# A mixture-of-experts block: the second-layer weight chunks go from SyncE's transfer queue to ScalarE's

## The chip, the cores and the metric

One core of one Trainium2 chip runs the whole program. The metric is the device time of one execution in microseconds (us); lower is better. The time before is the median of three runs.

## The reference

The block takes 512 tokens of width 1024, puts 16 meta tokens ahead of them, runs a convolution branch and an mLSTM branch over them and merges both (this first part is not touched by the change). Then comes a mixture of 32 experts, of which each token uses four:

```python
logits = xt @ router_w + router_b
top_val, top_idx = lax.top_k(logits, 4)
gates = softmax(top_val)
...
hcat = xb @ w1[e] + b1[e]                      # w1[e]: 1024 x 2048 float32, 8 MB
h_glu, h_lin = jnp.split(hcat, 2, axis=-1)     # clamped at 7, and at -7 and 7
act = h_glu * jax.nn.sigmoid(1.702 * h_glu) * (h_lin + 1.0)
return act @ w2[e] + b2[e]                     # w2[e]: 1024 x 1024 float32, 4 MB
```

The four results of a token are summed with their gates and added to the residual stream; a last RMS norm gives the output. All 32 experts' weights are read, 12 MB for each, 384 MB in all.

## The kernel before, in words

**The experts' loop.** The experts are worked off in order, one round of a loop for each, with up to 96 token slots for an expert in a pass. The number of passes comes from the data (`n_passes`); in the profiled execution there is one pass, with 32 rounds. The last round stands outside the loops of TensorE, VectorE and GpSimd, because it also starts the final sums.

**The weight ring.** An expert's weights are 12 chunks of 1 MB in 12 fixed buffers (`RING` = 12, L82). Chunks 0 to 7 are first-layer weights (`w1_ring`, `W1C` = 8, 128 rows of w1 each), chunks 8 to 11 second-layer weights (`w2_ring`, 256 rows of w2 each). The trace calls both `w_ring`. In every chunk each of the 128 partitions holds 8 KB that are contiguous in the chip's memory. There is one buffer for each chunk of an expert, so chunk c of the next expert can be asked for once TensorE has used chunk c of this one.

**TensorE's round** (`expert`, L1526 to 1593). It multiplies chunks 0 to 4 one after the other, each for three groups of 32 slots (L1539 to 1548), then two small bias products (L1552, L1558). Then it waits for chunks 5, 6 and 7 together (L1563, L1564) and works them off group by group (L1565 to 1570); this is called the late block below (`LATE` = 3). After that `second(t)` (L1572 to 1586) multiplies by the four w2 chunks, for slot groups 0, 1 and 2. It waits for the four chunks one by one within `second(0)` (L1579), and between `second(0)` and `second(1)` it transposes the next expert's tokens (L1591). A chunk is given free by `ring_used[c]` when its last product is done; for chunk 7 that is `hid_mm`, for chunk 11 `y_mm`. Chunks 8 to 11 are thus given free during `second(2)`, at the end of the round.

**SyncE's queue** (`load_block`, L528 to 536). It asks for the 12 chunks of the next expert in the order 0 to 11, and waits ahead of each for the buffer to be free; the routine that issues is `load_chunk` (L474 to 482, w1 at L478, w2 at L482). All 384 chunks go through SyncE's one hardware queue (q1 in the profile), in the order of the ring. Ahead of the loop the 12 chunks of expert 0 are loaded between other transfers (L488 to 500). SyncE then waits for the slot table (L519), reads it (L521, L524) and loads `last_g` (L526) before the first chunk of expert 1. After the loop it loads the experts' results (`load_results`, L540 to 548), and it has a branch for further passes (L556 to 561).

**ScalarE's round** (L1061 to 1081). It copies two biases out of the banks (L1065, L1067), picks a row (L1068), makes three sigmoids (L1073), waits for the transposes of the next tokens and copies them in two parts (L1080). It issues no transfer in this loop. Its own hardware queue (q10) was used earlier in the program, among others for eight 1 MB stores of zeros into `y_rows` (L884).

**GpSimd** sends each group's results to `y_rows` with an indirect transfer (L740) and gathers the tokens of the expert after next (L706), both through its software queue (q0).

Of the kernel before, what the change touches and what calls it, by code (L numbers as in the profile page):

```python
# [23 lines left out]
P = 128  # L24
# [6 lines left out]
TT = SEQ // P  # L31
# [13 lines left out]
NE = 32  # L45
# [31 lines left out]
TG = SLOTS // 32  # L77
# [4 lines left out]
RING = 12  # L82
W1C = KT
# [25 lines left out]
def hybrid_block(nc, x, meta_tokens, norm_mix_g, w_in, b_in, conv_dw_w, conv_dw_b, conv_ln_g, conv_ln_b,  # L109
# [3 lines left out]
    with ctx:  # L113
# [90 lines left out]
        w1_ring = [at(f"w1_ring{c}", [P, 2, DFF], F32, ring_end - chunk * (c + 1)) for c in range(W1C)]  # L204
        w2_ring = [at(f"w2_ring{c}", [P, 2, D], F32, ring_end - chunk * (W1C + c + 1)) for c in range(RING - W1C)]
# [159 lines left out]
        ring_in = [sem(f"ring_in{c}") for c in range(RING)]  # L365
        ring_used = [sem(f"ring_used{c}") if c not in (W1C - 1, RING - 1) else None for c in range(RING)]
# [3 lines left out]
        y_mm, y_made, y_stored, ffn_step = sem("y_mm"), sem("y_made"), sem("y_stored"), sem("ffn_step")  # L370
# [5 lines left out]
        summed, out_made, out_made_pool = sem("summed"), sem("out_made"), sem("out_made_pool")  # L376
# [41 lines left out]
        def out_parts(i):  # L418

            return [slice(0, D // 2), slice(D // 2, D)] if i == TILE_ORDER[-1] else [slice(0, D)]  # L420

        block = ctx.enter_context(nc.Block())

        @block.sync
        def _(sp):
# [47 lines left out]

            def load_chunk(e, c):  # L474

                if c < W1C:
                    src = expert_w1[0, bass.ds(e, 1), P * c:P * (c + 1), :].rearrange("e p (g n) -> p (e g) n", g=2)
                    sp.dma_start(w1_ring[c], src).then_inc(ring_in[c], 16)  # L478
                else:
                    m = c - W1C  # L480
                    src = expert_w2[0, bass.ds(e, 1), 2 * P * m:2 * P * (m + 1), :].rearrange("e (p k) n -> p (e k) n", p=P)
                    sp.dma_start(w2_ring[m], src).then_inc(ring_in[c], 16)  # L482

            sp.wait_ge(h_lo_made, 2 * TT)
            sp.dma_start(h_res, x[0].rearrange("(i p) d -> p i d", p=P)).then_inc(row_bc_in, 16)
            for c in range(4):  # L488
                load_chunk(0, c)
            load_pair(WO_PAIR, lambda s: w_source(WO_PAIR, s, 0))  # L490

            sp.wait_ge(mm_done, pair_tick(PW_PAIR + 1, 8))
            for c in range(4, 6):
                load_chunk(0, c)
            load_pair(WO_PAIR + 1, lambda s: w_source(WO_PAIR, s, 1))
# [3 lines left out]
            for c in range(6, RING):  # L499
                load_chunk(0, c)  # L500
            sp.dma_start(w_router, router_w[0].rearrange("(k p) e -> p k e", p=P)).then_inc(router_in, 16)
# [25 lines left out]

            def load_block(n, e):  # L528
                for c in range(RING):


                    if c in (W1C - 1, RING - 1):
                        sp.wait_ge(hid_mm if c < W1C else y_mm, n * TG)
                    else:
                        sp.wait_ge(ring_used[c], n)
                    load_chunk(e, c)

# [18 lines left out]
            with sp.If(passes > 1):  # L556
                with sp.Fori(1, passes) as q:
                    with sp.Fori(0, NE) as e:
                        sp.wait_ge(summed, q * TT + TT)
                        load_block(q * NE + e, e)  # L560
                    load_results(q)
# [223 lines left out]
        def _(act):  # L785
# [274 lines left out]
            with act.Fori(0, passes) as q:  # L1060
                with act.Fori(0, NE) as e:  # L1061
                    n = q * NE + e

# [15 lines left out]
                    for m in range(2):  # L1079
                        nc.scalar.activation(xT[:, 4 * m:4 * m + 4], banks[:, m, 0:4 * SLOTS].rearrange("p (k s) -> p k s", s=SLOTS),  # L1080
                                             ACT.Copy).then_inc(xT_made, 1)

            def last_square(m):
# [1047 lines left out]
```

## Time and profile before

| what | value |
|---|---|
| median of 3 runs | 1623.09 us |
| lowest and highest run | 1620.73 and 1624.62 us |
| the profiled execution's own time | 1621.82 us |
| span of its trace | 1620.0 us |
| mean granted clock of TensorE | 0.993 |
| TensorE busy with matmuls | 1580.6 us, 98% of the span |
| SyncE's queue q1 | 464.98 MB, 73.2% of the 16 DMA engines' span |
| chain that ended last | PE 82%, DMA 8%, each other engine 2% or less |

The span runs from the first instruction to the last one; 1.8 us of the execution's own time lie around it. PE is TensorE, DVE VectorE, ACT ScalarE, POOL GpSimd and SP SyncE; a q behind a name is that engine's sequencer, which issues transfers. L1532 is line 1532 of the kernel. "To landing" is the time from the issue of a transfer to the arrival of its last part. A row of a stretch gives its bounds, its length, the busy time of PE, weight loads, DVE, ACT and POOL with the number of instructions, and then TensorE's granted clock, the busy share of the 16 DMA engines (overlapping packets can bring it above 1) and GB/s. A row of a queue gives its packets, MB and the time of its packets as a share of 16 engines.

### The profile page before, as it was taken

The page shows a single profiled execution, that of the slowest core. Times are in us where ns is not written, and L with a number is a line of the kernel's source. Part 1 is how long each engine was busy: PE and PEld are TensorE (multiplying, and loading weights), DVE is VectorE, ACT ScalarE, POOL GpSimd, SP SyncE. Part 2 cuts the span into 40 slices and gives each one's busy share as a digit, 9 for nine tenths or more (in the row PEclk, how much of TensorE's full clock was granted, in tenths as well). Part 3 has the DMA queues.
Part 4 walks back from the last instruction along what each step waited for, and adds up shares of the span by engine and source line. Part 5 has one row for each costly group of instructions (what it writes and reads, how often), then busy time and mean ns, then how long its engine had stood idle before and what let it go on. Part 6 is the DMA issues. An engine that isn't in the chain of part 4 may idle for free.

```text
span 1620.0 us, 38897 instructions
## 1 busy us (share of the span) xinstructions
PE 1580.6 (98%) x16450; PEld 925.2 (57%) x16450; DVE 651.3 (40%) x1245; ACT 395.8 (24%) x605; POOL 427.9 (26%) x465
## 2 busy tenths in 40 slices
PE   6999999998999899999999999999999999999997
PEld 6998988876889634444444444334433444444444
DVE  4799898026241624222422242224222422242247
ACT  5333134255221511111111111111111111111112
POOL 7334334371433621211121112111211121112114
PEclk9999999999999899999999999999999999999999
DMA  7553243320275289999999999999999999999995
GB/s 215 157 182 105 79 144 90 105 78 27 78 298 212 84 300 411 408 409 414 413 408 403 410 411 406 406 409 410 399 409 406 411 395 402 407 411 400 400 416 243
DMA packets 132436, 492.91 MB, mean 304 GB/s; under 512 B 17305, under 2 KB 74817, under 8 KB 82628
## 3 DMA queue, kind: packets, MB, share of 16 engines
q1 hardware_dynamic: 114020, 464.98, 73.2%
q0 software_dynamic: 8736, 16.22, 3.1%
q10 hardware_dynamic: 9632, 11.03, 2.2%
q8 instruction: 35, 0.57, 0.2%
q14 instruction: 13, 0.11, 0.0%
HBM read 476.32 MB, written 24.87 MB: 309 GB/s over the span
## 4 chain that ended last, share of the span: by engine, by line
PE 82%; DMA 8%; POOL 2%; ACT 2%; DVE 2%; SPq 2%; issue 1%; POOLq 0%; DVEq 0%; ACTq 0%
PE banks L1532 36%; PE banks L1104 25%; PE banks L1581 17%; DMA w_ring<-in_expert_w_dram 7%; PE banks L1519 1%; POOL slot_table L693 1%; DVE mix_lo L1898 1%; SPq L442 1%; DMA small<-in_b_in_dram 0%; POOL h_res L759 0%; ACT banks L991 0%; ACT w_hi L800 0%; PE banks L1552 0%; ACT conv L954 0%; SPq L524 0%
## 5 line engine op out<-in xcount | busy, mean ns | idle before, releaser
L1532 PE MATMUL banks<-w_ring,xT 128*32 128x512 f32 x6144 | 671.5, 592 | 4.9 <-DMA w_ring<-in_expert_w_dram 4.0
L1532 PEld LDWEIGHTS banks<-w_ring,xT 128*32 128x32 f32 x6144 | 206.9, 110 | 429.9 <-issue 423.6
L1581 PE MATMUL banks<-w_ring,actT 128*32 128x256 f32 x6144 | 344.6, 380 | 0.0
L1581 PEld LDWEIGHTS banks<-w_ring,actT 128*32 128x32 f32 x6144 | 205.7, 110 | 134.3 <-issue 18.0
L2011 DVE TENSOR_TENSOR hid<-banks,bias 128x512 f32<-128x512 f32 x96 | 63.9, 665 | 477.4 <-PE banks L1532 477.4
L633 POOL TENSOR_TENSOR w_lo<-stage,w_hi 128x2048 fp32r<-128x2048 f32 x38 | 175.2, 4611 | 264.1 <-ACT w_hi L800 264.1
L1104 PE MATMUL banks<-u_hi,w_hi 128*128 128x264 f32 (+1 forms) x528 | 175.6, 333 | 0.3 <-ACT gates L914 0.3
L1104 PE MATMUL banks<-u_hi,w_lo 128*128 128x264 f32 (+1 forms) x528 | 174.6, 331 | 0.0
L1104 PE MATMUL banks<-u_lo,w_hi 128*128 128x264 f32 (+1 forms) x528 | 174.2, 330 | 0.0
L703 POOL COPY token_now<-token_of 96x1 int32 (+1 forms) x33 | 6.1, 183 | 568.7 <-PE banks L1519 564.9
L1065 ACT ACTIVATE bias<-banks 128x512 f32<-128x512 f32 x32 | 19.1, 597 | 560.5 <-PE banks L1552 560.5
L1722 DVE SCALAR_TENSOR_TENSOR banks<-conv_in,taps,banks 128x512 f32<-128x512 f32 x224 | 151.1, 749 | 0.1
L2037 DVE TENSOR_TENSOR y_out<-banks,bias 128x256 f32<-128x256 f32 x96 | 40.7, 424 | 228.5 <-PE banks L1581 228.4
L1104 PEld LDWEIGHTS banks<-u_hi,w_hi 128*128 128x128 f32 x528 | 99.2, 188 | 10.7 <-issue 0.9
L1104 PEld LDWEIGHTS banks<-u_lo,w_hi 128*128 128x128 f32 x528 | 99.2, 188 | 10.0
L1104 PEld LDWEIGHTS banks<-u_hi,w_lo 128*128 128x128 f32 x528 | 99.2, 188 | 9.5 <-issue 0.2
L800 ACT ACTIVATE w_hi<-stage 128x2048 fp32r<-128x2048 f32 x40 | 76.4, 1911 | 101.2 <-PE banks L1104 101.1
L740 POOL DMA_INDIRECT y_rows<-y_out,row_now x93 | 93.7, 1007 | 19.1 <-issue 19.1
L1073 ACT ACTIVATE sig<-hid 128x256 f32<-128x256 f32 x96 | 40.0, 416 | 202.2 <-DVE hid L2012 202.2
L2021 DVE TENSOR_TENSOR act_v<-hid,sig 128x256 f32<-128x256 f32 x96 | 60.5, 630 | 3.3
L712 POOL TENSOR_TENSOR carrier<-carrier 1x1 f32<-1x1 f32 x129 | 26.9, 209 | 95.9 <-DVE y_out L2037 92.4
L728 POOL COPY row_now<-row_of 128x3 int32 x32 | 5.8, 182 | 162.7 <-DMA y_rows<-y_out,row_now 161.4
(298 smaller groups left out, 1626.8 us busy)
## 6 DMA issues: line engine op xcount, KB each, us to landing
w_ring<-in_expert_w_dram SPq DMA_DIRECT2D x384, 1024.0 KB, 22.5
stage<-in_w_in_dram SPq DMA_DIRECT2D x20, 1024.0 KB, 5.3
stage<-in_w_in_dram SPq DMA_DIRECT2D x16, 512.0 KB, 5.3
y_rows<-empty_row ACTq DMA_DIRECT2D x8, 1024.0 KB, 4.7
y_in<-y_rows SPq DMA_DIRECT2D x4, 2048.0 KB, 22.4
stage<-in_conv_pw_w_dram SPq DMA_DIRECT2D x4, 1024.0 KB, 5.1
stage<-in_mlstm_out_w_dram SPq DMA_DIRECT2D x4, 1024.0 KB, 5.1
stage<-in_w_out_dram SPq DMA_DIRECT2D x4, 1024.0 KB, 5.5
```

Of the source, the lines that this page charges most:

```text
L633: nc.gpsimd.tensor_tensor(w_lo[:, s], stage[:, s], w_hi[:, s].bitcast(F32), ALU.subtract).then_inc(w_lo_made[s], 1)
L712: nc.gpsimd.tensor_tensor(carrier[:, 1 + i:2 + i], carrier[:, 0:1], carrier[:, 0:1], ALU.add).then_inc(idx_step, 1)
L740: pool.indirect_dma_start(out=y_dram, out_offset=bass.IndirectOffsetOnAxis(ap=row_now[:, t:t + 1], axis=0), in_=y_out[:, t], in_offset=Non ...
L800: nc.scalar.activation(w_hi[:, s], stage[:, s], ACT.Copy).then_inc(w_hi_made[s], 1)
L1073: nc.scalar.activation(sig[:, t], hid[:, t, 0:GRP], ACT.Sigmoid, scale=ALPHA).then_inc(sig_made, 1)
L1104: last = nc.tensor.matmul(dst, l, r, start=(k == 0 and n == 0), stop=(k == KT - 1 and n == 2))
L1532: last = nc.tensor.matmul(banks[32 * g:32 * (g + 1), t].rearrange("p (c j) -> p c j", j=64), xT[:, k, 32 * t:32 * (t + 1)], units, start=k ...
L1581: last = nc.tensor.matmul(banks[32 * g:32 * (g + 1), 3 + t, 0:GRP], actT[:, t, k], w2_ring[k // 2][:, k % 2, GRP * g:GRP * (g + 1)], start ...
L1722: nc.vector.scalar_tensor_tensor(out=to, in0=src, scalar=taps[:, ct, w:w + 1], in1=acc, op0=ALU.mult, op1=ALU.add).then_inc(conv_step, 1)
L2011: own(nc.vector.tensor_tensor(hid[:, t], banks[:, t], bias1.rearrange("p h n -> p (h n)"), ALU.add))
L2021: own(nc.vector.tensor_tensor(act_v[:, t].rearrange("p (c q j) -> p c j q", q=2, j=32), lin.rearrange("p (c j q) -> p c j q", q=2, j=32), ...
L2037: nc.vector.tensor_tensor(y_out[:, t], banks[:, 3 + t, 0:GRP], bias2, ALU.add).then_inc(y_made, 1)
```

## The change

`load_chunk` is moved out of SyncE's block and takes the issuing engine as its first argument. `load_block` on SyncE now issues chunks 0 to 7 only. ScalarE's round becomes a function `expert(n, e)`; the loop runs over the first 31 experts, and after each round ScalarE waits for the buffers 8 to 11 to be free and issues the w2 chunks of the next expert. The last round stands outside the loop. The 12 chunks of expert 0 are still issued by SyncE, and for a further pass SyncE issues the w2 chunks of expert 0 ahead of that pass. In a single pass, each chunk of experts 1 to 31 waits for the same event as before.

```diff
--- before.py
+++ after.py
@@ -419,6 +419,16 @@
 
             return [slice(0, D // 2), slice(D // 2, D)] if i == TILE_ORDER[-1] else [slice(0, D)]
 
+        def load_chunk(engine, e, c):
+
+            if c < W1C:
+                src = expert_w1[0, bass.ds(e, 1), P * c:P * (c + 1), :].rearrange("e p (g n) -> p (e g) n", g=2)
+                engine.dma_start(w1_ring[c], src).then_inc(ring_in[c], 16)
+            else:
+                m = c - W1C
+                src = expert_w2[0, bass.ds(e, 1), 2 * P * m:2 * P * (m + 1), :].rearrange("e (p k) n -> p (e k) n", p=P)
+                engine.dma_start(w2_ring[m], src).then_inc(ring_in[c], 16)
+
         block = ctx.enter_context(nc.Block())
 
         @block.sync
@@ -471,33 +481,21 @@
                 for j in range(2):
                     load_pair(stage_pair + j, lambda s: w_source(stage_pair, s, j))
 
-            def load_chunk(e, c):
-
-                if c < W1C:
-                    src = expert_w1[0, bass.ds(e, 1), P * c:P * (c + 1), :].rearrange("e p (g n) -> p (e g) n", g=2)
-                    sp.dma_start(w1_ring[c], src).then_inc(ring_in[c], 16)
-                else:
-                    m = c - W1C
-                    src = expert_w2[0, bass.ds(e, 1), 2 * P * m:2 * P * (m + 1), :].rearrange("e (p k) n -> p (e k) n", p=P)
-                    sp.dma_start(w2_ring[m], src).then_inc(ring_in[c], 16)
-
-
-
             sp.wait_ge(h_lo_made, 2 * TT)
             sp.dma_start(h_res, x[0].rearrange("(i p) d -> p i d", p=P)).then_inc(row_bc_in, 16)
             for c in range(4):
-                load_chunk(0, c)
+                load_chunk(sp, 0, c)
             load_pair(WO_PAIR, lambda s: w_source(WO_PAIR, s, 0))
 
             sp.wait_ge(mm_done, pair_tick(PW_PAIR + 1, 8))
             for c in range(4, 6):
-                load_chunk(0, c)
+                load_chunk(sp, 0, c)
             load_pair(WO_PAIR + 1, lambda s: w_source(WO_PAIR, s, 1))
 
             sp.wait_ge(mm_done, pair_tick(OW_PAIR + 1, 8))
             sp.wait_ge(mixed, KT)
             for c in range(6, RING):
-                load_chunk(0, c)
+                load_chunk(sp, 0, c)
             sp.dma_start(w_router, router_w[0].rearrange("(k p) e -> p k e", p=P)).then_inc(router_in, 16)
             sp.dma_start(rb_bc, router_b.to_broadcast([P, NE])).then_inc(router_in, 16)
             sp.dma_start(gf_bc, norm_ffn_g.to_broadcast([P, D])).then_inc(g_in, 16)
@@ -525,15 +523,15 @@
                                  by_slot[32 * t:32 * (t + 1)]).then_inc(rows_in, 16)
             sp.dma_start(last_g, final_norm_g.rearrange("(a d) -> a d", a=1).to_broadcast([P, D])).then_inc(row_bc_in, 16)
 
-            def load_block(n, e):
-                for c in range(RING):
+            def load_block(n, e, chunks=range(W1C)):
+                for c in chunks:
 
 
                     if c in (W1C - 1, RING - 1):
                         sp.wait_ge(hid_mm if c < W1C else y_mm, n * TG)
                     else:
                         sp.wait_ge(ring_used[c], n)
-                    load_chunk(e, c)
+                    load_chunk(sp, e, c)
 
             results = y_dram[0:Y_ROWS].rearrange("(i p r) n -> i p (r n)", i=TT, p=P)
 
@@ -555,6 +553,9 @@
             passes = sp.value_load(n_passes[0:1, 0:1], min_val=1, max_val=PASSES)
             with sp.If(passes > 1):
                 with sp.Fori(1, passes) as q:
+                    sp.wait_ge(summed, q * TT + TT)
+                    for c in range(W1C, RING):
+                        load_chunk(sp, 0, c)
                     with sp.Fori(0, NE) as e:
                         sp.wait_ge(summed, q * TT + TT)
                         load_block(q * NE + e, e)
@@ -1058,8 +1059,7 @@
             act.wait_ge(passes_made, 1)
             passes = act.value_load(n_passes[0:1, 0:1], min_val=1, max_val=PASSES)
             with act.Fori(0, passes) as q:
-                with act.Fori(0, NE) as e:
-                    n = q * NE + e
+                def expert(n, e):
 
                     act.wait_ge(bias_mm, n * 2 + 1)
                     nc.scalar.activation(bias1, banks[:, 3].rearrange("p (h n) -> p h n", h=2), ACT.Copy).then_inc(bias_made, 1)
@@ -1079,6 +1079,17 @@
                     for m in range(2):
                         nc.scalar.activation(xT[:, 4 * m:4 * m + 4], banks[:, m, 0:4 * SLOTS].rearrange("p (k s) -> p k s", s=SLOTS),
                                              ACT.Copy).then_inc(xT_made, 1)
+
+                with act.Fori(0, NE - 1) as e:
+                    n = q * NE + e
+                    expert(n, e)
+                    for c in range(W1C, RING):
+                        if c == RING - 1:
+                            act.wait_ge(y_mm, n * TG + TG)
+                        else:
+                            act.wait_ge(ring_used[c], n + 1)
+                        load_chunk(act, e + 1, c)
+                expert(q * NE + (NE - 1), NE - 1)
 
             def last_square(m):
```

## Rows read from the trace of the kernel before

**Rows 1.** The page: transfers over 40 slices, two queues, issues with us to landing.
```profile
DMA  7553243320275289999999999999999999999995
...
q0 software_dynamic: 8736, 16.22, 3.1%
q10 hardware_dynamic: 9632, 11.03, 2.2%
...
stage<-in_w_in_dram SPq DMA_DIRECT2D x20, 1024.0 KB, 5.3
```

**Rows 2.** The chain that ended last: start in us, length in us, work.
```profile
581.86 22.79 DMA w_ring<-in_expert_w_dram
604.79 7.93 PE banks L1532 x72
...
1026.00 7.73 PE banks L1532 x72
...
1058.23 7.73 PE banks L1532 x72
...
1544.56 7.93 PE banks L1532 x72
...
1577.47 7.73 PE banks L1532 x72
...
1606.16 6.42 POOL h_res L759 x2
```

**Rows 3.** The tile w_ring: what its readers waited for, and time to landing.
```profile
  DMA w_ring<-in_expert_w_dram: 4.0, 5
...
DMA to landing us min/median/max: 7.6/22.5/27.3
```

**Rows 4.** Stretches: all experts; one queue alone; beside GpSimd's. Last: clock, DMA share, GB/s.
```profile
604.00:1577.00 973.00, 970.40 (x11998) 415.88 (x12002) 280.32 (x645) 168.38 (x297) 153.68 (x300) 1.00 1.01 407
...
1018.00:1042.00 24.00, 24.00 (x300) 9.93 (x296) 8.65 (x20) 5.67 (x10) 2.76 (x6) 1.00 1.01 421
1010.00:1017.00 7.00, 7.00 (x96) 2.96 (x92) 0.42 (x1) 0.00 (x0) 2.28 (x4) 1.00 0.99 361
```

**Rows 5.** Timeline of TensorE, 1000 to 1036: start, us; one expert and its neighbours.
```profile
1005.68 7.11 PE L1581 MATMUL banks<-w_ring,actT 128*32 128x256 f32 x128
1012.61 13.06 PE L1532 MATMUL banks<-w_ring,xT 128*32 128x512 f32 x120
...
1025.81 7.91 PE L1532 MATMUL banks<-w_ring,xT 128*32 128x512 f32 x72
1033.54 2.77 PE L1581 MATMUL banks<-w_ring,actT 128*32 128x256 f32 x48
```

**Rows 6.** Timeline of SyncE, 1000 to 1070: start and length of each run of issues.
```profile
1010.40 2.92 SPq L482 DMA_DIRECT2D w_ring<-in_expert_w_dram  x4
1015.57 18.69 SPq L478 DMA_DIRECT2D w_ring<-in_expert_w_dram  x8
```

**Rows 7.** The issue of one last w2 chunk, and its time to landing.
```profile
L482 SPq DMA_DIRECT2D w_ring<-in_expert_w_dram x1: 332/332/332, 1013.0 to 1013.0; - x1
...
DMA to landing us min/median/max: 22.5/22.5/22.5
```

**Rows 8.** Timeline of ScalarE, 1000 to 1030: start, us; idle before.
```profile
1005.79 0.87 ACT L1080 ACTIVATE xT<-banks 128x384 f32<-128x384 f32 x2 [2.50 <-PE banks L1519]
...
1025.93 0.60 ACT L1065 ACTIVATE bias<-banks 128x512 f32<-128x512 f32 x1 [17.97 <-PE banks L1552]
```

**Rows 9.** Queues in the stretch 63 to 66, with both hardware queues at work.
```profile
q1 hardware_dynamic: 872, 0.44, 59.0%
q10 hardware_dynamic: 541, 0.55, 54.4%
```

**Rows 10.** Timeline of SyncE, 566 to 612: chunks for the second expert.
```profile
577.06 5.13 SPq L478 DMA_DIRECT2D w_ring<-in_expert_w_dram  x8
586.79 3.76 SPq L482 DMA_DIRECT2D w_ring<-in_expert_w_dram  x4
```

## The prediction

> **What bounds the kernel now.** I read the page first, for where the transfers are heavy: from the slice at about 600 us on, the 16 DMA engines are at 9 tenths in every slice but the last [rows 1]. That is the experts' loop. Then the chain of waits: it goes through TensorE's blocks, and at its beginning through a weight chunk that is 22.79 us under way and ends in the late block at 604.79 [rows 2]. The late block of the second expert (expert 1) starts at 604.79 and that of the last at 1577.47; that is 972.68 us for 30 rounds, 32.42 us each. The shortest rounds, such as that from 1026.00 to 1058.23, take 32.23 us [rows 2]. I take 32.23 us as TensorE's own round. Waiting for chunks thus costs 972.68 - 30 x 32.23 = 5.8 us in 30 rounds, 0.19 us each. The rows by tile count only 4.0 us in 5 waits [rows 3], expert 1's among them; smaller ones lie within the blocks.
>
> So there are two limits side by side. The windows show the second: from 604 to 1577 the DMA engines are busy for a share of 1.01 [rows 4], never free. With SyncE's queue alone they move 421 GB/s, beside GpSimd's transfers 361 GB/s [rows 4]. A chunk is 1.049 MB, 2.49 us at 421 GB/s; 12 of them take 29.9 us. The rest of the 32.42 us, 2.5 us, goes to GpSimd's stores and gathers. An expert's chunks take as long as TensorE's round, within 1%. Hence the median of 22.5 us to landing [rows 3]: some nine chunks stand in the queue, and one that comes late is made up for by nothing. What counts is the **order** in which they land.
>
> One round by the timelines: it starts at 1012.61, its late block at 1025.81, the second layer at 1033.54 [rows 5]. The four w2 chunks for it were asked for from 1010.40 to 1013.3, the w1 chunks of the next expert from 1015.57 on [rows 6]. The last w2 chunk, issued at 1013.0, lands 22.5 us later, at 1035.5 [rows 7]. TensorE comes to it after 3/4 of a group's second layer (7.11 / 2 = 3.6 us for a group [rows 5]), at 1033.54 + 2.7 = 1036.2: 0.7 us to spare. The late block's chunks are as tight.
>
> **The change, part by part.**
>
> *Issue time.* Four issues a round leave SyncE and go to ScalarE: 2.92 us from the first to the last, most of it waiting between them [rows 6]. SyncE is not late with w1: its next issue is at 1015.57, when chunk 0 comes free, and w2's waits end before that. So freeing it gains 0. On ScalarE what is queued behind the added waits is the bias copy of the next round. ScalarE ends its copies at 1006.7 and idles 17.97 us until 1025.93 [rows 8]; the w2 buffers come free by 1013, so the issues lie in that idle time, with 12 us to spare. Cost 0. If that cover were gone, VectorE's bias additions would be late, then the second layer. Around the end, ScalarE's last round issues nothing. Cost 0 too.
>
> *Order of landing.* Before, a w2 chunk stands behind all w1 chunks issued earlier. Afterwards it stands in q10, which has no backlog, and the DMA engines have two hardware queues to serve. No row has two streams of chunks side by side. The nearest is the stretch 63 to 66, with small packets: q1 takes 59.0% of the engines' time and q10 54.4% [rows 9]. I take equal shares. GpSimd's queue, which gets through in spite of q1's backlog (the rate falls to 361 in its stretch [rows 4]), speaks for the same.
>
> *The start.* SyncE comes late to expert 1: it issues all eight w1 chunks within 577.06 to 582.2, and w2's four from 586.79 on [rows 10]. Chunk 7 lands at 581.86 + 22.79 = 604.65, and TensorE starts its late block right then [rows 2]. At 586.79 w1 has 604.65 - 586.79 = 17.9 us to go, less the fixed part of a landing and GpSimd's share, still over five chunks. The four w2 chunks (9.96 us) therefore all get through on their half before chunk 7 does. Chunk 7 lands 10.0 us later, at 614.6. If TensorE then needs 32.23 us for each of 30 rounds, the last late block starts at 614.8 + 966.9 = 1581.7 instead of 1577.47: **+4.3 us**. The other 5.7 us come back since the chunks have a lead and the small waits vanish.
>
> *The steady state.* Total bytes and rate stay, so the DMA engines are as far as before at each time, unless they idle. At the time chunk 7 is needed, w2 chunks of the same expert have got ahead of it that stood behind it before. How many: w2 is issued from 1010.40, the late block starts at 1025.81 [rows 5, 6], 15.4 us, and both move together with TensorE. Of this take about 2.5 us for the fixed part of a landing (a lone 1 MB load takes 5.3 us [rows 1], less its 2.49) and 2.5 us for GpSimd's traffic, which falls in it: 10.4 us, of which q10 gets half, 5.2 us. So once the lead is used up the schedule lies **+5.2 us** behind that of before. The lead of 5.7 us shrinks by 0.19 us a round, so this limit is reached about the end. It is the larger of the two, and they don't add. The last chunk of w2: 4 x 2.49 x 2 = 19.9 us, plus 2.5 and 2.5, is 24.9 us after 1010.40, 1035.3, needed at 1036.2. No wait there, by 0.9 us.
>
> *The tail.* The results' loads follow TensorE and use the queue behind w1. The chain ends in output sums and scaling (the last long row at 1606.16 [rows 2]), all behind TensorE's last products. I carry the 5.2 us through it whole; from 0 (if loads bound it) to 6.
>
> *Rate.* What two streams do to the rate is the unknown. From below: the row nearest to a loss is 361 against 421 GB/s, 14%, but with small packets and stores [rows 4]; 14% over the some 18 us in which both are busy would be 3 us a round, 90 us in all. From above: a gain could at most remove all waits after the start, which the +4.3 us has already done. I take no loss, because packets of both streams are the same size and kind, and the busy share is 1.01 already. A 1% loss costs 0.18 us a round, some 5 us in all once the lead is gone. The Trainium skill (DMA: Bandwidth & Descriptors, Where 436 GB/s comes from) puts the ceiling of the ports at 435 GB/s. If a second queue filled the gap from the 421 measured, a chunk would take 2.41 us, the first wait 9.6 us, and the sum would be +3.9 instead of +5.2; no row shows this with chunks.
>
> **Sum**: the profiled execution's 1621.82 us + 5.2 = 1627.0. It lies 1.3 us under the median of the runs, so I predict 1623.09 + 5.2 = **1628.3 us**. A measurement of this kernel tells some 0.2% (3.2 us) from no change.
>
> **The rivals.**
>
> *A. Sharing costs rate* (1636 to 1650). If both streams together run 1.5 to 4% below 421 GB/s, 18 us of each round lengthen by 0.3 to 0.7 us, 8 to 22 us, beside the 5.2. For it: the fall to 361. Against: equal packets. Chance 0.19.
>
> *B. w2 becomes the late one* (over 1650). w2 has 0.9 us to spare. If q10 gets 40% and not 50%, its four chunks take 24.9 us instead of 19.9, TensorE waits 4 us for them in a round, and w1 gets ahead; with a full ring the DMA engines then run dry. A share of 45% or less of the time decides. 1 us lost a round is 30 us. For it: the small margin. Against: rows 9, where neither queue is starved. Chance 0.06.
>
> *C. The order doesn't change* (1623.1). If the engines serve chunks by time of issue whatever the queue, q10's wait behind q1's backlog, chunk 7 of expert 1 lands at 604.7, and SyncE's freed time is worth 0, as above. The Trainium skill (DMA: Bandwidth & Descriptors, Issuing engines are not separate DMA queues) says that DMAs of all issuers interleave on the same engines and that issuing from several saves the sequencers' time only; by that alone the sum would be 0. Against it: rows 9 show both at once. Chance 0.12.
>
> *D. Faster* (1617.3). C's order at the start, and the rate of both queues over 0.6% higher, so that the chunks take less than TensorE's 32.23 us: all 5.8 us of waits go. It is decided by whether chunk 7 of expert 1 lands by 604.8. For it: 0.6% is little. Against: needs the order and the gain both. Chance 0.07.
>
> The forecast itself (1625 to 1631) has 0.56.
>
> **How the numbers follow.** The likeliest time is 1628.3. The range from 1622.0 to 1642.0 holds the forecast, C, and the lower half of A, and leaves out D, B and the rest of A, 0.2 or less. Slower by over 0.2%: A, B and most of the forecast (0.81 less 0.04 where it ends just under the bound), 0.77. Same: C and that 0.04, 0.16. Faster: 0.07.
>
> **What would show it.** In the profile after: expert 1's late block starts at about 614.6, released by chunk 7, some 33 us after its issue; w2 chunks land about 9 us (the first) to 22 us (the last) after issue, in q10, which carries some 130 MB more than before; the following rounds take 32.2 us with no DMA wait, w1's times to landing start low and grow; the last late block starts near 1582.5. A start at 604.7 would prove C or D; rounds of 32.6 us or more with a DMA share of 1.01 and below 405 GB/s A; waits ahead of the second layer and a DMA share under 1 B. Any w1 issue that SyncE makes earlier relative to TensorE would prove the first part wrong.

## The result: 9.5 us slower

The median after is 1631.91 us (1630.41 to 1633.92, five runs) beside 1622.40 us (1620.73 to 1624.62, five runs) before. The ratio is 1.0058, with a 95% interval of 1.0044 to 1.0073, so the kernel is slower by 0.4 to 0.7%. The forecast was 5.2 us slower.

The page after, where it answers to [rows 1]:

```profile
span 1632.1 us, 38925 instructions
...
DMA  7553242320275299999999999999999999999994
...
q1 hardware_dynamic: 96164, 334.95, 52.6%
q10 hardware_dynamic: 27488, 141.06, 22.2%
...
L1543 PE MATMUL banks<-w_ring,xT 128*32 128x512 f32 x6144 | 672.8, 593 | 15.6 <-DMA w_ring<-in_expert_w_dram 14.6
...
L729 POOL COPY row_now<-row_of 128x3 int32 x32 | 5.8, 181 | 208.2 <-DMA y_rows<-y_out,row_now 206.9
```

130 MB moved from q1 to q10, and the DMA engines are at 9 tenths from the same part of the span on as before. Work on TensorE is as long as before (its first-layer products are line 1543 here, the second layer is line 1592). What grew is its wait for chunks, and GpSimd's wait for its own stores to land: 206.9 us over 31 rounds, where the same group (line 728 there) had 161.4 us before.

The chain, to be laid beside [rows 2] (start, length, work):

```profile
580.69 32.23 DMA w_ring<-in_expert_w_dram
613.05 9.29 PE banks L1543 x72
...
646.85 7.73 PE banks L1543 x72
...
1324.04 7.97 PE banks L1543 x72
1332.16 24.87 DMA w_ring<-in_expert_w_dram
1357.16 7.97 PE banks L1543 x72
...
1574.03 25.47 DMA w_ring<-in_expert_w_dram
1599.54 1.07 PE banks L1592 x16
```

Chunk 7 of expert 1 is 32.23 us under way instead of 22.79, and the late block waits for it. Then some 22 rounds go through TensorE alone, until chunks come into the chain again from 1332 on. At the very end a w2 chunk is in it, 25.47 us under way. The last late block starts at 1587.33, so the profiled execution can be cut in three:

| part | before | after | difference |
|---|---|---|---|
| to expert 1's late block | 604.79 | 613.05 | +8.26 |
| from it to the last late block, 30 rounds | 972.68 | 974.28 | +1.60 |
| from there to the end of the span | 42.53 | 44.77 | +2.24 |
| span | 1620.0 | 1632.1 | +12.1 |

This execution took 1633.92 us, 2.0 us more than its median, and that of before 0.6 us less than its own; so 12.1 us are seen where the medians differ by 9.5.

TensorE's timeline shows the first and the last part of this (start, length, instructions, idle before):

```profile
613.05 9.29 PE L1543 MATMUL banks<-w_ring,xT 128*32 128x512 f32 x72 [9.85 <-DMA w_ring<-in_expert_w_dram]
...
1599.54 1.07 PE L1592 MATMUL banks<-w_ring,actT 128*32 128x256 f32 x16 [1.71 <-DMA w_ring<-in_expert_w_dram]
```

The late block itself takes 9.29 us instead of 7.93. The stretches tell why (columns as in [rows 4]; last come granted clock, DMA share, GB/s):

```profile
604.00:613.00 9.00, 0.00 (x0) 0.00 (x0) 0.00 (x0) 1.39 (x3) 0.00 (x0) 0.59 1.02 422
613.00:622.00 9.00, 8.95 (x72) 2.81 (x76) 4.50 (x11) 0.83 (x2) 0.00 (x0) 0.84 1.01 422
640.00:1290.00 650.00, 650.00 (x8056) 266.59 (x8052) 182.50 (x420) 113.37 (x200) 102.64 (x201) 1.00 1.01 405
1300.00:1587.00 287.00, 283.55 (x3514) 123.08 (x3510) 83.77 (x192) 46.63 (x83) 46.09 (x90) 1.00 1.00 401
```

While TensorE idles the granted clock falls to 0.59, and it is 0.84 over the late block: part of the block runs at the lower of its two levels, 1.2 GHz. The third line is to be read beside the same 650 us of before, where TensorE was also busy throughout, and the fourth beside the end of the loop before:

```profile
640.00:1290.00 650.00, 649.86 (x8039) 276.40 (x8032) 185.34 (x427) 113.78 (x201) 102.44 (x200) 1.00 1.01 408
1300.00:1577.00 277.00, 275.33 (x3382) 118.72 (x3378) 80.46 (x185) 45.34 (x80) 43.53 (x85) 1.00 1.01 404
```

The DMA engines look full in all four, yet move 405 GB/s instead of 408, and 401 instead of 404 at the end of the loop, where both kernels wait for chunks. By the queues' rows the engines are not quite as busy: the shares of the queues add up to 101.3% before and 100.9% after in the 650 us.

The queues in the 16 us from 590 on, in which both hardware queues have chunks at work:

```profile
DMA packets 1018, 6.73 MB, mean 421 GB/s; under 512 B 166, under 2 KB 166, under 8 KB 226
...
q1 hardware_dynamic: 449, 3.26, 49.0%
q10 hardware_dynamic: 441, 3.23, 48.3%
q0 software_dynamic: 128, 0.25, 4.0%
```

Equal shares, at the 421 GB/s of one queue alone [rows 4].

### The profile page after: what moved, and what is told of

It reads as the page before. It is cut to its first block, busy times and chain, and to the rows that moved or that the text cites. A ratio compares the mean times of both kernels' runs of the same rounds, so it can differ in the third digit from the quotient of the medians.

```text
span 1632.1 us, 38925 instructions
## 1 busy us (share of the span) xinstructions
PE 1579.1 (97%) x16450; PEld 913.0 (56%) x16450; DVE 652.9 (40%) x1245; ACT 392.9 (24%) x603; POOL 428.0 (26%) x465
## 4 chain that ended last, share of the span: by engine, by line
PE 77%; DMA 13%; DVE 2%; ACT 2%; POOL 2%; SPq 2%; issue 1%; POOLq 0%; DVEq 0%; ACTq 0%
PE banks L1543 33%; PE banks L1115 25%; PE banks L1592 16%; DMA w_ring<-in_expert_w_dram 13%; PE banks L1530 1%; POOL slot_table L694 1%; DVE mix_lo L1909 1%; SPq L452 1%; DMA small<-in_b_in_dram 0%; ACT banks L992 0%; ACT w_hi L801 0%; ACT conv L955 0%; POOL h_res L760 0%; SPq L522 0%; PE banks L1563 0%
## 5 line engine op out<-in xcount | busy, mean ns | idle before, releaser
L1543 PEld LDWEIGHTS banks<-w_ring,xT 128*32 128x32 f32 x6144 | 202.2, 110 | 445.3 <-issue 437.5
L1592 PEld LDWEIGHTS banks<-w_ring,actT 128*32 128x32 f32 x6144 | 199.2, 110 | 143.0 <-issue 18.7
L729 POOL COPY row_now<-row_of 128x3 int32 x32 | 5.8, 181 | 208.2 <-DMA y_rows<-y_out,row_now 206.9
```

Of the source, the lines that this page charges most:

```text
L1543: last = nc.tensor.matmul(banks[32 * g:32 * (g + 1), t].rearrange("p (c j) -> p c j", j=64), xT[:, k, 32 * t:32 * (t + 1)], units, start=k ...
L1592: last = nc.tensor.matmul(banks[32 * g:32 * (g + 1), 3 + t, 0:GRP], actT[:, t, k], w2_ring[k // 2][:, k % 2, GRP * g:GRP * (g + 1)], start ...
```

## The experiments

Two theories stood against each other. **Order**: the w2 chunks of an expert overtake w1 chunks asked for before, which costs once, at the start. **Rate**: two hardware queues side by side move less, which costs in each round. Smaller suspects were ScalarE's issues and waits, and the last w2 chunk. Each of the three series of runs was made on a chip of its own (by their numbers 1, 7 and 4), and the medians of the kernel before differ between them (1628.62, 1630.91 and 1622.02 us). So each experiment is read against the kernel before of its own series. The times in us that the expectations of the first two series name start from the 1622 us of the result and are too low by 6 to 9 us for that reason; what can be held against them is the difference. Runs of one kernel lie up to 9 us apart (e2: 1632.50 to 1641.37), so one trace explains a median only within a few us.

| run | median us | ratio to before, 95% interval | expert 1's late block: wait, length |
|---|---|---|---|
| *first series, before 1628.62* | | | |
| e1, ScalarE waits but issues nothing | 1629.17 | 1.0005 [0.9995, 1.0014] | 0.6, 7.93 |
| e2, only the first w2 by ScalarE | 1637.17 | 1.0052 [1.0036, 1.0068] | 9.94, 10.24 |
| e3, only the first w2 by SyncE | 1637.77 | 1.0056 [1.0043, 1.0070] | none; expert 2: 6.66, 10.57 |
| e4, only the last w2 by SyncE | 1640.45 | 1.0074 [1.0061, 1.0087] | 6.9, 9.94 |
| *second series, before 1630.91* | | | |
| e5, early chunks, one queue | 1634.25 | 1.0023 [1.0008, 1.0038] | none |
| e6, early chunks, two queues | 1633.24 | 1.0018 [1.0007, 1.0029] | none |
| l1, light products, one queue | 1620.72, one run | | |
| l2, light products, two queues | 1625.33, one run | | |
| *third series, before 1622.02* | | | |
| b, the kernel before again | 1621.35 | 0.9997 [0.9985, 1.0009] | 0.98, 7.93 |
| a, the changed kernel again | 1628.29 | 1.0039 [1.0024, 1.0054] | 10.45, 10.33 |
| e8, half of the first w2 by ScalarE | 1625.40 | 1.0016 [1.0004, 1.0028] | 4.86, 10.41 |
| e7, two early chunks, one queue | 1616.42 | 0.9969 [0.9956, 0.9982] | none |

**e1_scalar_waits_only.** The changed kernel, but SyncE issues all 12 chunks, and ScalarE only waits for the buffers.

```diff
-            def load_block(n, e, chunks=range(W1C)):
+            def load_block(n, e, chunks=range(RING)):
...
                             act.wait_ge(ring_used[c], n + 1)
-                        load_chunk(act, e + 1, c)
```

> ScalarE waits for the w2 buffers at the end of its round as in the changed kernel, but issues nothing; SyncE issues all 12 chunks as before. If the cause is the queue (order of landing and rate), this is the kernel before: about 1622.4 us, within 0.2%, and the late block of the second expert starts at about 604.8. If ScalarE's added waits or its restructured loop cost the time, it comes out near the changed kernel's 1631.9.

The interval of the ratio holds 1, as expected, and the chain at its start is like that of before:

```profile
583.61 22.27 DMA w_ring<-in_expert_w_dram
606.02 7.93 PE banks L1539 x72
```

The restructured loop and ScalarE's waits cost nothing that can be measured. In the changed kernel itself the issues are covered too, as its ScalarE timeline shows at expert 0:

```profile
585.78 2.93 ACTq L430 DMA_DIRECT2D w_ring<-in_expert_w_dram  x4
...
603.13 0.60 ACT L1065 ACTIVATE bias<-banks 128x512 f32<-128x512 f32 x1 [12.70 <-PE banks L1563]
```

**e2_first_w2_by_scalar.** The four w2 chunks of expert 1 go through ScalarE's queue, all others through SyncE's.

```diff
+            load_block(1, 1, range(W1C))
+            with sp.Fori(2, NE) as e:
                 load_block(e, e)
...
+                expert(q * NE, 0)
+                w2_loads(q * NE, 0)
+                with act.Fori(1, NE) as e:
+                    expert(q * NE + e, e)
```

> Only the second expert's four w2 chunks go through ScalarE's queue, all later ones through SyncE's. Theory (order and rate): the second expert's late block starts about 9 us late, at about 613; then SyncE's queue alone has a lead that it loses by 0.19 us a round, so all 30 further rounds take 32.24 us; the end is set by TensorE and comes 9.3 us later, plus 1.4 for the block at a lower clock, less the 5.8 us of small waits: about +4.9, 1627.3 us. Rival 'the start sets all': 1632. Rival 'nothing but the lower rate of two queues counts': 1622.

```profile
584.27 32.46 DMA w_ring<-in_expert_w_dram
616.87 10.24 PE banks L1543 x72
```

Four transfers of 124 give the long wait, 9.94 us, and +0.52% of time (+8.5 us). The expectation was +4.9 us, with 5.8 us of small waits coming back; the result is nearer to its rival, that the start sets all. On this chip TensorE's round is longer (see the last section), so the kernel has few small waits, and nothing comes back. The unedited changed kernel was not timed in this series; against e4 below, which is that kernel but for one expert, +8.5 us are most of the cost. It sits in one place, the start.

**e3_first_w2_by_sync.** The reverse: the first four w2 chunks by SyncE, those of experts 2 to 31 by ScalarE.

```diff
+            load_block(1, 1, range(RING))
+            with sp.Fori(2, NE) as e:
                 load_block(e, e)
...
+                expert(q * NE, 0)
+                with act.Fori(1, NE - 1) as e:
+                    expert(q * NE + e, e)
+                    w2_loads(q * NE + e, e)
```

> The reverse: the second expert's w2 chunks stay in SyncE's queue, those of all later experts go through ScalarE's. Theory: no long wait at the start (late block of the second expert at 604.8), but the third expert's late block comes some 5 us late, later rounds wait for chunks all along, and the end is the same as with the change, since the transfers set it: 1631 to 1632 us. Rival 'the start sets all': 1622 to 1625.

```profile
614.52 31.24 DMA w_ring<-in_expert_w_dram
645.90 10.57 PE banks L1544 x72
```

The long wait does not go; it moves one expert on, to the first one whose w2 uses the second queue, and is then the only one (6.66 us). With the slow block behind it (10.57 us instead of 7.93) that is 9.3 us, and the medians differ by 9.1 us. So the expected number came, but not for the reason given with it: no later round waits for a chunk, TensorE's rounds are its own. On this chip the cost belongs to the passage from one queue to two, whenever that comes, not to the steady state.

**e4_last_w2_by_sync.** The w2 chunks of expert 31 go back to SyncE.

```diff
-            with sp.Fori(1, NE) as e:
+            with sp.Fori(1, NE - 1) as e:
                 load_block(e, e)
+            load_block(NE - 1, NE - 1, range(RING))
```

> As changed, but the last expert's w2 chunks are issued by SyncE, ahead of the results' loads in the same queue. Theory: the wait of 1.7 us ahead of the last w2 chunk goes, and the last late block isn't held by w2 any more (0.5 us at most): 1629.7 us, 2.2 us less than changed. If the results' loads beside w2 cost nothing: 1631.9.

It has the full cost, +11.8 us, and its only wait for a chunk is the one at the start, 6.9 us. The expected gain of 2.2 us can't be seen: in e3, whose last w2 chunks still go through ScalarE's queue, no w2 chunk is late at the end either, and the unedited changed kernel was not timed beside it. Whether SyncE's queue would take the 1.71 us away where they occur stays open. The wait and the slow block (9.94 us) make 8.9 us; why the median is 11.8 us above is not explained either.

**e5_early_one_queue and e6_early_two_queues.** Four w1 chunks of expert 1 are issued as soon as they come free, ahead of SyncE's wait for the slot table; e5 with one queue, e6 with the change's two (the edit of e6 is shown, that of e5 is the same on the kernel before).

```diff
+            for c in range(4):
+                sp.wait_ge(ring_used[c], 1)
+                load_chunk(sp, 1, c)
...
-            with sp.Fori(1, NE) as e:
+            load_block(1, 1, range(4, W1C))
+            with sp.Fori(2, NE) as e:
```

> The kernel before, with the second expert's first four w1 chunks issued by SyncE ahead of its wait for the slot table, when their buffers come free. Theory that what counts is how far transfers are ahead: chunk 7 of the second expert lands about 7 to 10 us earlier, the wait of 2.4 us goes and the small waits of all later rounds with it: rounds of 32.24 us throughout, about 1616.6 us (-0.36%). Rival: the table's reads come later behind the chunks and delay the second expert's gather: 1622 or more.

> The same early chunks in the changed kernel. Theory: the transfers set its end, and four chunks (10 us) are done earlier: about 10 us less than changed, 1622 us, still slower than the early version with one queue. If only the order at the start counted, it would reach that version's 1616.6.

With the transfers ahead of TensorE, neither has a wait for a chunk, and the two intervals lie over each other: a cost of two queues can't be seen then. TensorE's round is the long one in this series, about 32.6 us, so a small loss of rate would stay hidden. Both are nevertheless slower than before, where 0.36% less (e5) and about the time of before (e6) were expected: a miss, by the rival that e5's expectation names. In e5 the fourth early chunk is issued only at 569.3, and the slot table is read at 573.80, 17.2 us after the first expert product instead of 13.1 in the kernel before. VectorE waits for that table ahead of its bias additions, and TensorE pays for it at expert 0:

```profile
581.49 5.35 PE L1585 MATMUL banks<-w_ring,actT 128*32 128x256 f32 x64 [3.75 <-issue]
```

In e6 the same place costs 1.78 us. Four early chunks were too many; e7 below takes two.

**l1_light_one_queue and l2_light_two_queues.** To look at the rate where chunks and not TensorE set the pace, both leave out most first-layer products of slot groups 1 and 2; l1 with the loads of before, l2 with those of the change. The same products of the late block are replaced by one small product each.

```diff
-                        for t in range(TG):
-                            last = hidden(k, t)
+                        last = hidden(k, 0)
```

> Leaves out most first-layer products of slot groups 1 and 2, so TensorE's round needs about 19 us and the transfers alone set the pace; all chunks in SyncE's queue. A round then shows what one expert's transfers take: 32.4 us expected (12 x 2.49 plus 2.5 for GpSimd's), 421 GB/s where SyncE's queue is alone. If GpSimd's part is hidden in a longer TensorE round, less than 32.

> The same lightened kernel with w2 in ScalarE's queue. Theory that two queues lower the rate by 0.7 to 1%: rounds longer than with one queue by 0.2 to 0.35 us, 6 to 10 us over the loop. Rival, that the rate is the same and order alone costs: rounds equal within 0.05 us.

The queues of l1 over 920 us, then those of l2:

```profile
DMA packets 56639, 374.92 MB, mean 408 GB/s; under 512 B 9041, under 2 KB 9085, under 8 KB 12665
...
q1 hardware_dynamic: 49471, 360.26, 96.2%
```

```profile
DMA packets 56411, 372.91 MB, mean 405 GB/s; under 512 B 9054, under 2 KB 9098, under 8 KB 12687
...
q1 hardware_dynamic: 32653, 237.87, 63.2%
q10 hardware_dynamic: 16523, 120.34, 32.3%
```

2.01 MB less in the same 920 us, 0.54%, is 0.17 us in a round of 32.3 us, or 5 us in 30; 6 to 10 were expected. The spans differ by 4.7 us (1618.9 and 1623.6), but 2.3 of these lie ahead of the first expert product (560.1 and 562.4). Counted from it the last product of the second layer starts 5.2 us later (1591.9 and 1599.4). GpSimd's wait for its stores is 161.6 us in l1 and 191.6 us in l2. This is one execution each, but the loss has the same sign and size in the pair of the result (265.33 MB before and 263.56 MB after in 650 us, 0.67%).

What the loss is made of stays open. With q0 (4.8% and 5.0%) the queues' shares add up to 101.0% in l1 and 100.5% in l2. So the engines' packets took about as long per MB in both, and the engines had a little less under way: moments in which too few chunks stand in the queues would look like this too, and no run tells them from slower transfers.

**b_before_again and a_after_again.** Both kernels unedited, on one chip and in one series. It was not the chip of the earlier experiments, as the expectations suppose.

> The kernel before once more, with a profile, on the chip of the other runs, where it took 1628.6 us and the first experiment's rounds took 32.58 us with next to no waits. Expected: rounds of 32.6 us, time to landing of some 18 us, late block of the second expert 46 to 48 us after the first expert's start, as in the run in which ScalarE only waits.

> The changed kernel with a profile on the same chip. If the one long wait of the second expert is what costs there, it is slower by 9 to 11 us (0.6 to 0.7%), with rounds as long as before's after it. If two queues cost in every round there too, rounds are longer than before's and the loss is over 15 us.

Neither expectation came quite true: b's rounds take 32.43 us on the mean and not 32.6, with 22.4 us to landing and not 18, and a is slower by less than 9 us. The chains of b and of a:

```profile
583.29 21.95 DMA w_ring<-in_expert_w_dram
605.38 7.93 PE banks L1532 x72
...
1578.28 7.73 PE banks L1532 x72
```

```profile
579.96 31.85 DMA w_ring<-in_expert_w_dram
611.94 10.33 PE banks L1543 x72
...
1582.22 7.73 PE banks L1543 x72
```

The experts' products began at 558.8 in b and at 555.6 in a (tile w_ring), so expert 1's late block starts 46.6 us later in b and 56.3 us later in a: **+9.7 us**. The 30 rounds then take 972.90 us in b and 970.28 us in a, -2.6. The rest of the span is 42.6 and 42.7 us. The sum, +7.2, meets the medians (1628.29 less 1621.35, +6.9). The two profiled spans differ by 4.0 us only, because a came to its first expert product 3.2 us earlier. In a, no wait for a chunk follows the first one, and the median to landing is 10.0 us:

```profile
  DMA w_ring<-in_expert_w_dram: 10.5, 1
```

and the DMA share from 640 to 1290 is 0.99 at 406 GB/s: the lead won by the long wait was never used up. TensorE sets the pace there, so a does not show whether two queues could move less: at the end of the loop (1300 to 1577) it moves 406 GB/s, where b moves 404. The slow block shows in a's stretches:

```profile
601.00:612.00 11.00, 0.55 (x16) 0.19 (x12) 0.00 (x0) 2.26 (x4) 0.00 (x0) 0.75 1.01 422
612.00:622.00 10.00, 10.00 (x72) 2.86 (x76) 4.57 (x11) 0.83 (x2) 0.00 (x0) 0.76 1.02 424
```

10.33 us instead of 7.93 are 2.4 us, the price of having idled 10.45 us ahead of it, at a granted clock of 0.76.

**e8_half_of_first_w2_by_scalar.** As e2, with two chunks instead of four in ScalarE's queue.

```diff
+            load_block(1, 1, [*range(W1C), RING - 2, RING - 1])
...
+                for c in range(W1C, RING - 2):
+                    act.wait_ge(ring_used[c], q * NE + 1)
+                    load_chunk(act, 1, c)
```

> Half the dose: of the second expert's four w2 chunks only the first two go through ScalarE's queue, everything else through SyncE's. Theory (each w2 chunk that gets ahead delays chunk 7 by its 2.5 us): the late block of the second expert starts some 5 us later than before's, half of the 9 to 10 us seen with four, and the kernel is 0.25 to 0.3% slower than before. If the wait came from anything else about ScalarE's issuing, it would be all of it or nothing.

```profile
582.67 27.31 DMA w_ring<-in_expert_w_dram
610.11 10.41 PE banks L1537 x72
```

Expert 1's late block starts 51.6 us after the first expert product (at 558.5), 5.0 us later than in b: two overtaking chunks, 2 x 2.49 us. Half the dose gives half the delay. The time, +0.16%, is below the expected 0.25 to 0.3%, which its interval just reaches. The block is as slow as after the full wait, 10.41 us, though the wait was 4.86 us: that price is not in proportion to the wait.

**e7_two_early_one_queue.** The kernel before, with chunks 0 and 1 of expert 1 issued ahead of SyncE's wait for the slot table. This tests the other side of the theory: give the queue a lead instead of taking one away.

```diff
+            for c in range(2):
+                sp.wait_ge(ring_used[c], 1)
+                load_chunk(1, c)
...
-            with sp.Fori(1, NE) as e:
+            load_block(1, 1, range(2, RING))
+            with sp.Fori(2, NE) as e:
```

> The kernel before with only two of the second expert's w1 chunks issued ahead of the wait for the slot table. With four of them the table's last scatters landed 4 us later and VectorE waited 3.8 us for the table. With two, both chunks have landed by 569 and the table isn't late; chunk 7 lands 5 us earlier. Expected: no DMA wait at the second expert, 2.5 us or a little less gained on this chip (-0.1 to -0.15%). If the table is late again: 0 to +0.2%.

SyncE's timeline, then the chain (it goes through TensorE alone):

```profile
558.11 2.92 SPq L478 DMA_DIRECT2D w_ring<-in_expert_w_dram  x2
```

```profile
600.91 7.73 PE banks L1536 x72
...
1568.68 7.73 PE banks L1536 x72
```

30 rounds take 967.77 us, 32.26 us each, where b took 972.90: all waits for chunks are gone. This kernel beats both, by 5.6 us (0.3%) against before, where 2.5 us or less were expected. The slot table is read 13.1 us after the first expert product, as in b. Chunk 0 is issued 2.8 us after the first expert product, in b 20.2 us after it. The early chunks with the change's two queues were not tried in this series. e7 also confirms in another way that waiting for chunks cost the kernel before some 5 us.

## Why the prediction was right in sign and short in size

**Issue time, 0.** Right, by e1 and by ScalarE's 12.70 us of idle time left.

**Order of landing, equal shares.** Right: 49.0% and 48.3%. Rival C, by which the order would not change, is refuted by e2, e3 and e8. The Trainium skill (DMA: Bandwidth & Descriptors, Issuing engines are not separate DMA queues) says that the transfers of all issuers interleave on the same engines, and that issuing from several saves sequencer time only. The trace agrees with both: the two queues share, and no run with two queues was faster. But to interleave is to overtake: ScalarE's chunks landed ahead of SyncE's older ones, and chunk 7 took 32.23 us instead of 22.79. So "the sum would be 0" did not follow.

**The start, chunk 7 10.0 us later.** Right within 0.7 us. Counted from the first expert product (556.7 before, 555.7 after), expert 1's late block is 9.3 us later, and 9.7 us in the pair a and b. The predicted 614.6 was 613.05, for the larger part because the loop began a microsecond earlier.

**The rest of the start, +4.3 net.** This step was short by a missing term. That TensorE's granted clock falls while it waits, and that the late block after it runs partly at the lower level, was not in the sum; it measured 1.4 us in the profiled execution and 2.4 to 2.5 us in a and e8. With it the start alone is 9.7 + 2.4 - 5.1 = +7.0 us, which is what a against b shows (+7.2). The 5.1 us that come back are those predicted as 5.7.

**The steady state, lead used up about the end, and the schedule then 5.2 us behind.** On the pair of the result the lead was used up by 1332, some 22 rounds on and not 30, and the last late block starts 9.9 us behind that of before (1587.33 and 1577.47), 10.9 us counted from the first expert product. The shrinking itself came as foretold: SyncE's chunks take 11.9 us to landing (median) from 640 to 770 and 17.8 us from 1290 to 1420, while in a they stay at 10.0 and 10.2. What failed there is **Rate**: "no loss" was wrong, by 0.5 to 0.7%, near the 1% case that the text had priced at some 5 us. An estimate from these numbers: 0.5 to 0.7% of 973 us are 4.9 to 6.8 us, and the gap is 5.7. That the order alone would give the 5.2 us was never measured by itself. Where only chunks are at work the rate stays at 421 GB/s as argued. It is with GpSimd's stores and gathers beside both hardware queues that less is moved. The 10 us of this traffic in one round, before and then after:

```profile
1008.00:1018.00 10.00, 10.00 (x144) 4.42 (x136) 0.85 (x2) 0.00 (x0) 3.38 (x5) 1.00 1.00 379
```

```profile
1016.00:1026.00 10.00, 10.00 (x143) 4.31 (x135) 0.85 (x2) 1.28 (x1) 3.26 (x5) 1.00 1.01 373
```

Over 28 rounds, from 18 to 8 us ahead of each late block, the mean is 375 GB/s before and 366 after; in the rest of the round it is 421 and 422. The loss lies in the first five of these ten us (364 and 337 GB/s, at a DMA share of 1.00 and 0.97; in the second five it is 386 and 394), in which SyncE has not yet asked for the next expert's chunk 0. This speaks for engines short of chunks there rather than for slower transfers, but it was not tried.

In the 30 rounds the small waits are not gone: 974.28 - 967.8 (30 undisturbed rounds, from e7) - 1.4 for the slow block leaves 5.1 us of them. In run a they stayed away, and why the lead lasted there and not in the result's execution is open. Rival A named this loss, but as 1.5 to 4%, and placed it in the stretch of both hardware queues.

**The last w2 chunk, no wait by 0.9 us, and the tail carried whole.** Right in a. In the profiled execution of the result this margin did not hold: the chunk needed 25.5 us instead of the 22 predicted, and TensorE waited 1.71 us. SyncE had issued the results' loads beside it (its timeline):

```profile
1580.82 13.14 SPq L546 DMA_DIRECT2D y_in<-y_rows  x4
```

That they are the cause was argued and not shown: in a they were issued beside it too (from 1574.98 on), and its last w2 chunks landed within 12.6 us of their issue.

**Sum.** For the profiled execution: +9.3 and +1.4 at the start, less 1.0 for the earlier beginning, +0.2 in the small waits (5.1 instead of 4.9), +2.2 in the tail: +12.1 us. For a against b: +7.2. The measured +9.5 between the medians of the result lies between them; which of its runs used up the lead is not to be seen without their traces. The forecast of +5.2 had the direction, and the order as the cause, right. Of the two terms that it lacked, it had left out the slow block (1.4 to 2.6 us in the runs) and taken the loss of rate as nothing. The measured 1631.9 lies just above the forecast's own band of 1625 to 1631 and is inside the stated range through the room left there for rival A. Two small slips of its arithmetic (1581.7 less 1577.47 is 4.2, and 5.3 less 2.49 is 2.8, taken as 2.5) move it by 0.2 us at most. Rivals B and D did not occur: only the very last of the w2 chunks held TensorE's products up, and no run with two queues was faster than before.

## What to carry to other kernels

When one queue is always full, what matters is the order in which its transfers land. A second queue gives what goes through it about half of the engines at once (48.3% here), and it is paid for by the older transfers that the consumer needs first. Put on a second queue only what is needed sooner than what waits in the first, or look at the place where the queue's lead is lost, and issue there earlier: here two chunks asked for some 17 us sooner gained 5.6 us.

## What the runs showed of the hardware beyond this

- With both hardware queues and GpSimd's at work 0.5 to 0.7% less was moved in two pairs of executions (405 instead of 408 GB/s over 650 us); whether the transfers are slower or too few is open. GpSimd's waits for its stores grew there from 161.4 to 206.9 us in 31 rounds, 1.5 us each, and from 161.6 to 191.6 us from l1 to l2. Where the chunks had a lead, these waits were the same with one queue in the loop (e2 175.7, e5 171.7 us) as with two (a 171.6, e3 171.8 us).
- In e8 a wait of 4.86 us (and one of 0.92 us a block earlier) ahead of the late block made it as slow (10.41 us) as one of 10.45 us (10.33 us), while one of 9.85 us (with one of 1.61 us a block earlier) gave 9.29 us. The length of the wait does not set the price in these three.
- In the first two series, on other chips than the third, TensorE's own round was longer. Around 1000 us the same 64 products of the second layer took 3.64 us in b and 3.98 us in e1, and the first layer's weight loads were busy for 205.8 us in b and 377.7 us in e1, at a granted clock of 1.00 in both. No wait is named that would explain it. A round 0.3 us longer leaves the chunks time to keep up, so there the small waits are gone before any change, and with them what the long wait gives back: e2 cost 8.5 us there, the change 6.3 to 6.9 us in the third series. Why the products run in another rhythm in those series was not settled; the chip is one difference, and neither of the two kernels was traced on those chips.
